# A tile region moved to 128 modulo 512 bytes, a mask product in one pass, and two heads' value products taken in turns, in a three-block transformer kernel

## The reference, cut to what matters

```
x = first_block(x)      # 12 dilated heads, 8 banded (window 128) query heads on 2 kv heads,
                        # two sigmoid gates, squared-relu MLP of 4096
for l in 0, 1:
    x = x + 0.5 * swiglu(rms_norm(x))              # width 1408
    c = rms_norm(x) @ w_in + b_in
    y = stick_breaking(c), mlstm(c), mla(c)        # three branches of 4 heads
    x = x + (gate-weighted sum of the three, projected) @ w_out
    x = x + 0.5 * swiglu(rms_norm(x))
```

## Time and profile before

| | |
|---|---|
| median of 3 runs | 2558.68 us |
| lowest and highest | 2553.43, 2560.25 us |
| the profiled execution | 2553.38 us, span 2551.6 us |
| mean granted TensorE clock | 0.992 |
| PE busy | 2500.7 us (98% of the span), 11206 records |
| DVE, ACT, POOL busy | 48%, 37%, 52% |
| DMA | 27% of the 16 engines, 83 GB/s |
| chain that ended last | 84% PE, 9% DVE, 3% issue |

### The profile page before, as it was taken

How to read it: one execution, slowest core, us unless ns; L and a number is a source line. 1 busy time by engine, 2 the same in 40 slices (tenths; PEclk the granted TensorE clock), 3 DMA queues, 4 the chain that set the end, 5 groups by cost and what they waited for, 6 DMA issues and landing times.

```text
span 2551.6 us, 29209 instructions
## 1 busy us (share of the span) xinstructions
PE 2500.7 (98%) x11206; PEld 1993.3 (78%) x11206; DVE 1227.6 (48%) x1972; ACT 938.6 (37%) x1495; POOL 1315.6 (52%) x1593
## 2 busy tenths in 40 slices
PE   8999989999999999999999999999999999999999
PEld 7777868888888888676677888888886767878887
DVE  4667656433224532358644743333323695357331
ACT  4444443322223223443534432332335354254321
POOL 4535236656556555344434665555542562457554
PEclk9999999999999999999999999999999999999999
DMA  5211113333333333112112333333331221223333
GB/s 176 75 34 58 50 59 91 99 99 91 99 99 104 100 92 104 58 50 66 59 58 87 95 94 97 99 92 99 99 98 34 66 67 50 76 85 97 98 93 98
DMA packets 59610, 213.38 MB, mean 84 GB/s; under 512 B 6608, under 2 KB 6736, under 8 KB 59344
## 3 DMA queue, kind: packets, MB, share of 16 engines
q1 hardware_dynamic: 59472, 211.52, 27.4%
HBM read 209.39 MB, written 2.10 MB: 83 GB/s over the span
## 4 chain that ended last, share of the span: by engine, by line
PE 84%; DVE 9%; issue 3%; POOL 2%; ACT 2%; DMA 0%; SPq 0%; DVEq 0%; POOLq 0%; ACTq 0%
PE banks L659 83%; POOL t L1796 2%; DVE t L1496 1%; DVE t L1359 1%; DVE t L1501 1%; DVE t L997 1%; DVE t L1092 1%; DVE t L1098 1%; ACT t L1543 1%; DVE t L1195 1%; DVE t L999 1%; PE banks L768 0%; POOL t L1804 0%; DVE t L1108 0%; DVE t L1001 0%
## 5 line engine op out<-in xcount | busy, mean ns | idle before, releaser
L659 PE MATMUL banks<-t,t 128*128 128x512 f32 (+6 forms) x10854 | 2468.9, 391 | 36.5 <-POOL t L1796 18.0
L659 PEld LDWEIGHTS banks<-t,t 128*128 128x128 f32 (+2 forms) x10854 | 1952.6, 189 | 516.9 <-issue 93.4
L1796 POOL TENSOR_TENSOR t<-t,t 128x256 fp32r<-128x256 f32 x1548 | 1260.6, 845 | 1210.1 <-ACT t L1543 1210.1
L1543 ACT ACTIVATE t<-t 128x1024 fp32r<-128x1024 f32 x387 | 410.0, 1060 | 1160.0 <-issue 608.6
L1092 DVE TENSOR_TENSOR t<-banks,t 128x512 f32<-128x512 f32 x121 | 83.5, 690 | 222.3 <-PE banks L659 222.2
L1252 DVE TENSOR_TENSOR t<-banks,t 128x512 f32<-128x512 f32 x44 | 30.4, 691 | 183.5 <-PE banks L659 183.4
L1220 DVE SCALAR_TENSOR_TENSOR t<-banks,t 128x512 f32<-128x512 f32 x32 | 22.1, 692 | 157.9 <-PE banks L659 157.9
L981 DVE SCALAR_TENSOR_TENSOR t<-t,t,t 128x512 fp32r<-128x512 f32 x64 | 51.4, 803 | 61.9 <-ACT t L1552 61.9
L1197 DVE TENSOR_TENSOR t<-t,t 128x512 fp32r<-128x512 f32 x68 | 71.7, 1054 | 2.3
L1226 DVE TENSOR_TENSOR t<-banks,t 128x512 f32<-128x512 f32 x24 | 16.6, 692 | 107.3 <-PE banks L659 107.3
L1247 DVE TENSOR_TENSOR t<-banks,t 128x512 f32<-128x512 f32 x44 | 30.4, 692 | 70.4 <-PE banks L659 70.0
(11 more groups left out here) (160 smaller groups left out, 1272.2 us busy)
## 6 DMA issues: line engine op xcount, KB each, us to landing
t<-in_w SPq DMA_DIRECT2D x387, 512.0 KB, 3.6
t<-in_xT SPq DMA_DIRECT2D x8, 256.0 KB, 6.1
out<-t SPq DMA_DIRECT2D x8, 256.0 KB, 3.8
t<-in_dmask SPq DMA_DIRECT2D x1, 1536.0 KB, 11.5
t<-in_vbias SPq DMA_DIRECT2D x2, 384.0 KB, 3.9
t<-in_c SPq DMA_DIRECT2D x1, 576.0 KB, 8.1
t<-in_pos SPq DMA_DIRECT2D x2, 256.0 KB, 5.9
t<-in_smask SPq DMA_DIRECT2D x1, 256.0 KB, 11.7
```

What stands on the lines that cost most here:

```text
L659: return pe.matmul(o, l, r, start=start, stop=stop, skip_group_check=True)
L1543: a.activation(whl[u % 2][:, 0:1024], wraw[u % 3][:, :], ACT.Copy).then_inc(*w_high.next(u))
L1796: p.tensor_tensor(hl[:, 1024:2048][:, c], wraw[u % 3][:, c], as_f32(hl[:, c]), ALU.subtract).then_inc(*w_low.next((u, q)))
```

## The change

```diff
@@ memory
-        rcol_t = take(8)
         cst = take(128 * len(CONSTS))
...
         top[0] += 4 * KB
+        R0 = top[0]
+        top[0] += 110 * KB
         pg2_t = take(256)
+        mask_r = take(256, F32R)
+        vb_t = take(768)
+        rcol_t = take(8)
         cols_t = take(NCOL + 7)
         small_t = take(112)
         m2 = small_t[:, 0:32]
-        vb_t = take(768)
-        R0 = -(-top[0] // 64) * 64
@@ swa_values
-                for hf in range(2):
-                    for k in range(2):
+                for k in range(2):
+                    for hf in range(2):
                         ins = mm(B[ba][64 * hf:64 * hf + 64, 0:128], VB[:, k0 + k, 64 * hf:64 * hf + 64],
@@ sb_scores
-                    mm(B[bk][:, 0:128], C["ident"], C["m01s"], False, True).then_inc(...)
+                    mm(B[bk][:, 0:128], mask_r[:, 0:128], mask_r[:, 128:256], False, True).then_inc(...)
@@ consts
-                v.tensor_scalar(C["m01s"], C["m01s"], -1.0, 1e30, A_, M_).then_inc(*v_norm.next())
+                v.tensor_copy(mask_r[:, 0:128], C["ident"]).then_inc(*v_norm.next())
+                v.tensor_scalar(mask_r[:, 128:256], C["m01s"], -1.0, 1e30, A_, M_).then_inc(*v_norm.next())
```

More of the change, by code:

```diff
@@ L527, in build_program @@
         m2 = small_t[:, 0:32]
-        vb_t = take(768)
-        R0 = -(-top[0] // 64) * 64
         def reg(kb, cols_, dt=F32):
             return at(R0 + int(kb * KB), cols_, dt)
-        assert base + R0 + 110 * KB <= nc.sbuf_usable_end, (base + R0 + 110 * KB - nc.sbuf_usable_end)
         def col(name, i=0):
@@ L828, in sb_scores @@
                     mm(B[bk][:, 0:S - 128 * j], SBK[t_][rows, 128 * j:128 * j + 128], SBQ[t_][rows, 128 * j:S], True, False)
-                    mm(B[bk][:, 0:128], C["ident"], C["m01s"], False, True).then_inc(*t_attn.next(("sb_z", l, h, j)))
+                    mm(B[bk][:, 0:128], mask_r[:, 0:128], mask_r[:, 128:256], False, True).then_inc(*t_attn.next(("sb_z", l, h, j)))
                     bank[bk] = [(v_attn, ("sb_keep", l, h, j))]
```

## The result

| | before | changed |
|---|---|---|
| median | 2558.68 us (2553.43 to 2560.47, 5 runs) | 2531.8 us (2528.17 to 2535.2, 5 runs) |
| profiled execution: own time, span | 2553.38, 2551.6 us | 2535.2, 2533.3 us |
| mean granted clock of that execution | 0.992 | 0.992 |

The direction was right; the forecast size was half of what came.

What follows compares the result with a forecast made beforehand. PE, busy for 98% of the span, was taken as the bound. Terms 6.8 + 5.0 + 0 + 1.8 = 13.6 us off the profiled 2553.4 gave 2539.8, as a median 2545 us; own range 2536 to 2551, widened to 2536 to 2556.

Steps and rivals of the forecast that it cites:

- Part 1: Tile region moved to 128 modulo 512: 3000 products go from 0.2289 to the 0.2267 us of `xs_t`, 6.8 us.
- The first rival: Operand place is not the cause of 0.2267 against 0.2289, something else in second matmuls is: about 2552 us; chance 0.14.
- Part 2: 32 attention masks in one pass: 0.15 us less before a score, 0.17 before a dense product, 5.0 us.
- Part 3: Heads in turns in `swa_values`: column halves already run side by side, so 0; bound 0.8 us gained or 7 lost.
- Both rivals on the turns: In `swa_values`, turns break the column halves' overlap, about 2552 us, or gain up to 7 us, 2538; chance 0.02 each.
- Part 4: New order of stick-breaking items: values of heads 0 and 1 become neighbours, 0.9 us in each of 2 layers, 1.8 us.
- The rivals had it fall more often: In the mixers, shorter masks and moved items make the granted clock fall more often: about 2551 us; chance 0.04.
- the rival that it was widened for: Range widened to 2556 for most of the rival of PE stalling at `sb_values`, about 2567 us; chance 0.03.
- this rival: PE reaches `sb_values` before DVE and ACT are done and stalls, a wait replacing the gain: about 2567 us; chance 0.03.

Runs made afterwards that it cites:

- e1: Kernel before with only the tile region moved to start at 128 modulo 512: 2548.95 us against 2555.36, ratio 0.9978.
- e16: Kernel before with the whole layout 64 bytes on, so weights, `xs_t` and region all start at 192 modulo 512: 2549.37 us.
- e15: Kernel before with the region at 128 modulo 512 and the weight tiles moved from 128 to 192, `xs_t` staying at 128: 2595.48 us.
- e2: Kernel before with masks in one float32r pass, the planner keeping the old price and so the old order: 2549.67 us, ratio 0.9976.
- e8: Changed kernel with the mask's old price in the planner, so without the new order: 2544.14 us against 2554.71 for the kernel before, ratio 0.9964.
- e4: Kernel before with only the two heads taken in turns in `swa_values`: 2554.81 us, ratio 0.9998.
- e3: Kernel before with the new order alone: the planner prices masks as cheap while they stay float32 in two records: 2541.93 us, ratio 0.9949.
- e7: Kernel before with head 0's values held for head 1's and line 864's transposes 6 dense products later: 2541.82 us, ratio 0.9949.
- e5: Kernel before with the planner holding stick-breaking head 0's values until head 1's are ready, in each layer: 2547.08 us, ratio 0.9967.
- e6: Kernel before with the transposes of line 864 placed behind 6 more dense products in each layer: 2549.28 us, ratio 0.9978.
- e9: Changed kernel with the transposes of line 864 placed behind 6 more dense products in each layer: 2531.83 us, ratio to before 0.9899.

## Why the prediction was right or wrong

**Part 1, 6.8 us: right.** 6.4 us by `e1`, all of it full-speed time, and 0.2267 in every region stretch. The step that gave the region the pace of `xs_t` held, but its wording, that 128 modulo 512 is the fast place, did not: `e16` is as fast at 192, and `e15` slow at 128. The first rival (the place is not the cause) fell by `e1`. With it fell, for this kernel, the fixed gap that the Trainium skill, TensorE: Matmul & The Clock Gate (Back-to-back issue gap), states: the same product took 0.2267 to 0.2334 us by its operands' places.

**Part 2, 5.0 us: right, a little high.** `e2` gives 4.1 us of full-speed time. The forecast had 0.27 us to the next score and 0.17 to a dense product, and the profile 0.25 and 0.16. The rest of its 5.7 us is clock, which `e8` doesn't repeat.

**Part 3, 0: right.** `e4`: 0.5 us, with an interval of the ratio that takes in 1, and by the timeline 0.3 us, within the forecast's bound of 0.8. Both rivals on the turns fell, and with the second one what the Trainium skill, TensorE: Matmul & The Clock Gate (Part 3), says of strict order, for column halves in this kernel.

**Part 4, 1.8 us: wrong, and together with the clock (below) the reason for the miss.** `e3` gives 13.4. Two things in that step failed, and a third was sized too low.
- "The wait of line 864 for DVE stays about as it is". It went from 2.43 to 1.33 us a layer, from the start of the product ahead of it. The forecast had PE arrive earlier by 4.3 us and guessed DVE's scans earlier by as much. In fact DVE was ready sooner still.
- The wait of the column sums, 2.7 us behind line 1001, was in the same view as the earlier trace rows and wasn't read. It is 1.73 us a layer before and 0.32 in the new order, since DVE no longer has `conv` steps ahead of `rsqrt`. The forecast looked at PE's order only, where the products hardly move; DVE's order had it. `kup`, late next, took some 2 us of it back.
- The value pairs were sized well (3.87 us each). The changes of shape around them were worth somewhat more than the 0.2 us taken: some 1.5 us a layer with the pair instead of 0.9.

That makes 5.9 us of full-speed time instead of 1.8; the 4.1 more are a third of the miss of 13.3 us. Parts 1 and 2 gave 1.3 us less than forecast, which hides as much of it.

**The clock, 7.5 us: not in the sum at all.** The rivals had it fall more often, at 0.04, and no case had it fall less often. Yet the row for 1154 to 1172 us showed both halves of it, PE waiting and the clock at 0.91, and in the same trace the falls stood right behind waits. A forecast of less waiting should have carried a term for the clock: 20.5 us of the mixers ran at half clock in before's profile, 10 us lost, and by `e3` and `e7` 5.5 to 7.5 us of such loss go with the new order or its shorter waits. How a wait brings a fall about stays open. What is left of the miss is mostly the spread of the medians, some 2 us (before was at 2558.68 in its own five runs and at 2555.36 in the 27); 0.9 us of full-speed time the whole has over the sum of its parts, which no run explains.

**The range.** Its own terms (-3.3, -3.8 and -5 us, +1.6 and +2, around 2545) add to 2533 to 2549, not to the 2536 to 2551 that the prediction has, and the rival that it was widened for, at 2552, is the first and not the second. The measured 2531.8 lies below either.

**The rivals.** No wait took the gain's place at `sb_values`: the pair ends in 3.87 us. A wait did come back at `kup`, 2.8 us, of the kind that this rival named and at another place.

## What to carry to other kernels

Where two kinds of the same product run at two paces, compare where both operands start, not only the one that differs, and try a shift of a tile before anything else: it is one line. A price in a planner is part of a change, so time the new order by itself, and price every wait whose surroundings move, from the whole view of waits. Where waits of 2 us sit in a stretch in which the clock falls, a wait taken away may give its own length again in clock (as in `e5` and `e6`) or none (`e9`), so say what the sum would be with and without it.

## What the runs showed of the hardware that was not expected

- A float32r product of 512 columns takes 0.2267, 0.2289 or 0.2333 us by the distance, modulo 256 bytes, between the starts of weights and moving operand. With every such product at the wrong distance, some 9300 by the plan, the kernel took 46 us more (`e15` against `e16`). That is less than the 62 us that 0.0067 us each make; where the rest went is not shown.
- A multiple of 128, 256 or 512 bytes is no good by itself: at 0 and at 256 modulo 512, with the weights at 128, the kernel was 10 us slower than before.
- In the mixers the clock falls mostly in or right behind short waits, 65 of 69 times: behind 21 of 28 waits of 2.3 us or more at line 864 and none of 10 of 1.1 to 1.3 us there, but behind 17 of 66 of 0.9 to 1.3 us elsewhere. It also fell four times without one, once after 27 us in which PE was busy all the time.
- With the same program the time lost to the clock differs by several us: 10.2 to 17.1 us in the first 600 us of 20 profiles.
